# Score masking and its row maxima in one pass per head, and a reordered gating piece, in a two-layer hybrid decoder kernel

## The reference

```python
h = rms_norm(x, norm1)
z = h @ w_in                       # split into za, bq, bk, bv, cq, ck, cv, cg
a_out = causal_spatial_gating(gelu(za), a_ln_g, a_ln_b, a_ws, a_bs)
b_out = dilated_attention(bq, bk, bv)        # 8 heads of 64
c_out = silu(cg) * groupnorm(retention(rotary(cq), rotary(ck), cv))
x = x + concat(a_out, b_out, c_out) @ w_out
x = x + hier_moe(rms_norm(x, norm2), ...)    # 16 experts of 3 x 2 MB, fp32

def causal_spatial_gating(z, ...):           # z = gelu(za)
    u, v = split(z)
    vn = layer_norm(v) * ln_g + ln_b
    s = tril(w_s) @ vn + b_s                 # over 128 tokens, 4 groups
    return u * s
```

## Time and profile before

| | us |
|---|---|
| median of 3 executions | 717.48 |
| lowest, highest | 714.62, 717.77 |
| span of the profiled execution | 714.6 |

### The profile page before, as it was taken

The page is one execution under the profiler, slowest core; times in us unless marked ns, Lnnn a source line. Parts: engine busy times, 40 slices in busy tenths (PEclk is TensorE's granted clock), DMA queues, the critical chain, the costliest instruction groups (busy, mean ns, idle before and its releaser), DMA issues.

```text
span 714.6 us, 9124 instructions
## 1 busy us (share of the span) xinstructions
PE 670.8 (94%) x3452; PEld 384.6 (54%) x3452; DVE 308.9 (43%) x605; ACT 191.9 (27%) x342; POOL 16.3 (2%) x29
## 2 busy tenths in 40 slices
PE   6998999999999999998999989999999999999984
PEld 5877778733543543542388768785353453453431
DVE  3479886711331321321474798865131331231224
ACT  3438434311201201201154445442111111111102
POOL 3000000200000000000020000000000000000000
PEclk9999999999999999999999999999999999999998
DMA  9974039999999999999986330898999999999991
GB/s 334 341 276 168 1 137 389 372 421 404 422 406 394 422 421 421 421 421 421 402 285 223 130 118 30 328 389 338 424 403 423 403 423 415 421 422 419 421 414 63
DMA packets 46026, 240.95 MB, mean 337 GB/s; under 512 B 3457, under 2 KB 3649, under 8 KB 21281
## 3 DMA queue, kind: packets, MB, share of 16 engines
q1 hardware_dynamic: 44800, 238.21, 82.8%
q0 software_dynamic: 1040, 2.04, 1.1%
q10 hardware_dynamic: 144, 0.13, 0.1%
HBM read 239.32 MB, written 1.05 MB: 336 GB/s over the span
## 4 chain that ended last, share of the span: by engine, by line
PE 74%; DMA 10%; DVE 8%; ACT 4%; issue 2%; SPq 1%; DVEq 0%; PEldq 0%; ACTq 0%
PE psum L1059 28%; PE psum L746 14%; PE psum L1091 14%; DMA up_w<-in_w_up 7%; PE psum L1043 4%; DMA down_w<-in_w_in 3%; PE psum L1004 3%; PE psum L766 2%; ACT xT L671 1%; PE psum L973 1%; DVE scores L1200 1%; PE psum L1071 1%; PE psum L914 1%; PE psum L731 1%; DVE scores L1182 1%
## 5 line engine op out<-in xcount | busy, mean ns | idle before, releaser
L746 PE MATMUL psum<-piece_hi,hT_part 128*128 128x512 f32 x416 | 130.2, 394 | 3.4 <-ACT gate_b L611 1.5
L1059 PE MATMUL psum<-up_w,xT 128*64 128x512 f32 x512 | 113.3, 594 | 4.9 <-DMA up_w<-in_w_up 4.9
L1091 PE MATMUL psum<-down_w,scores 128*64 128x512 f32 x512 | 113.5, 595 | 0.6 <-ACT scores L680 0.6
L746 PEld LDWEIGHTS psum<-piece_hi,hT_part 128*128 128x128 f32 x416 | 76.7, 188 | 21.0 <-issue 5.8
L746 PE MATMUL psum<-piece_lo,hT_part 128*128 128x512 f32 x208 | 81.2, 391 | 0.0
L1059 PEld LDWEIGHTS psum<-up_w,xT 128*64 128x64 f32 x512 | 37.7, 137 | 76.7 <-issue 68.2
L1091 PEld LDWEIGHTS psum<-down_w,scores 128*64 128x64 f32 x512 | 36.6, 137 | 64.7 <-issue 63.1
L1495 DVE TENSOR_TENSOR y_lo<-psum,y_hi 128x512 fp32r<-128x512 f32 x32 | 22.1, 691 | 110.9 <-ACT y_hi L687 110.9
L1059 PE MATMUL psum<-gate_a,xT 128*64 128x512 f32 x256 | 56.6, 593 | 1.2 <-DMA gate_a<-in_w_gate 1.2
L1059 PE MATMUL psum<-gate_b,xT 128*64 128x512 f32 x256 | 56.4, 593 | 0.0
L1474 DVE SCALAR_TENSOR_TENSOR work<-work,psum 128x512 f32<-128x512 f32 x16 | 11.0, 687 | 100.8 <-ACT work L678 100.8
(11 more groups left out here) (234 smaller groups left out, 763.2 us busy)
## 6 DMA issues: line engine op xcount, KB each, us to landing
up_w<-in_w_up SPq DMA_DIRECT2D x32, 2048.0 KB, 13.7
down_w<-in_w_down SPq DMA_DIRECT2D x64, 1024.0 KB, 11.7
gate_b<-in_w_gate SPq DMA_DIRECT2D x32, 1024.0 KB, 13.0
gate_a<-in_w_gate SPq DMA_DIRECT2D x32, 1024.0 KB, 15.9
up_w<-in_w_in SPq DMA_DIRECT2D x6, 2048.0 KB, 13.4
down_w<-in_w_in SPq DMA_DIRECT2D x4, 2048.0 KB, 21.3
down_w<-in_w_out SPq DMA_DIRECT2D x4, 2048.0 KB, 7.8
up_w<-in_w_in SPq DMA_DIRECT2D x4, 1024.0 KB, 8.4
```

The lines of the kernel that those rows point to most:

```text
L746: ins = pe.matmul(o, src[a][:, c, t * P:(t + 1) * P], w[b][:, c, :], start=(c == 0 and n == 0), stop=(c == DC - 1 and n == len(parts) - 1))
L1059: ins = pe.matmul(psum[e * SLOTS:(e + 1) * SLOTS, bank, :], xT[:, c, k:k + SLOTS], w[:, e, c, :], start=(c == 0), stop=(c == DC - 1))
L1091: ins = pe.matmul(psum[e * SLOTS:(e + 1) * SLOTS, 2 + n, :], heT[:, c, e * SLOTS:(e + 1) * SLOTS], down_w[:, e, c, n * COLS:(n + 1) * COLS ...
```

## The change

- `mask` and `score_max` become one: for each head and token tile one `tensor_tensor_reduce` that adds a table to the products, multiplies by `q_scale`, writes `scores`, and keeps the minimum of what it wrote. `q_scale` is now negative, so that `scores` hold the negated masked scores and the minimum is the negated maximum. The exponentials take `scale=-1.0`. The table `logq` is `logc` divided by the (positive) scale, made once per layer by two instructions, with `q_inverse` (one small instruction) for it.
- `masked` is signalled by each of the eight instructions instead of once, and the eight exponentials each wait for their own.
- ScalarE takes `exps(0)` ahead of the tanh of the gating piece; `split_hi(CVG)` follows the tanh.
- VectorE takes `norm_probs(0)` right behind `gelu_arg`, ahead of the wait for the tanh; `split_lo(CVG)` goes ahead of the layer norm's statistics; the cosines go ahead of the wait for the spatial product; `split_lo(BV, 0)` goes behind `mask(1)`.
- TensorE does the spatial product in the middle of CVG (in `swap_score`) instead of ahead of it.

```diff
+        q_inverse = sb("q_inverse", [P, T])
+        logq = sgate.rearrange("p t n -> p (t n)")[:, 0:3 * P]
-        scored, masked, exped = signal("scored", 2), signal("masked", 2), signal("exped", 2)
+        scored, masked, exped = signal("scored", 2), signal("masked", 16), signal("exped", 2)
...
-                    act.wait_ge(masked.sem, masked.at(l, k + 1))
                     for j in heads:
-                        act.activation(scores[:, j, 0:P], scores[:, j, 0:P], ACT.Exp, bias=nmax[:, k, j:j + 1],
+                        act.wait_ge(masked.sem, masked.at(l, 8 * k + 2 * j + 1))
+                        act.activation(scores[:, j, 0:P], scores[:, j, 0:P], ACT.Exp, bias=nmax[:, k, j:j + 1], scale=-1.0,
                                        accum_out=denom[:, k, j:j + 1])
+                        act.wait_ge(masked.sem, masked.at(l, 8 * k + 2 * j + 2))
...
+                exps(0)
                 act.wait_ge(gelu_arg.sem, gelu_arg.at(l, 1))
                 act.activation(work1[:], work0[:], ACT.Tanh, ...).then_inc(gelu_tanh.sem, 1)
-                exps(0)
                 split_hi(CVG)
...
-                pe.wait_ge(vn_ready.sem, vn_ready.at(l, 1))
-                for g in range(4):
-                    ins = pe.matmul(psum[:, 7, :]..., wsT[:, g, :], za[...], start=True, stop=True)
-                ins.then_inc(spatial_done.sem, 1)
                 def swap_score():
+                    pe.wait_ge(vn_ready.sem, vn_ready.at(l, 1))
+                    for g in range(4):
+                        ins = pe.matmul(psum[:, 7, :]..., wsT[:, g, :], za[...], start=True, stop=True)
+                    ins.then_inc(spatial_done.sem, 1)
                     pe.wait_ge(proj_copied_a.sem, proj_copied_a.at(l, CQK))
...
-                pe.wait_ge(masked.sem, masked.at(l, 2))
+                pe.wait_ge(masked.sem, masked.at(l, 16))
...
-                    for b in range(2):
-                        link(V.scalar_tensor_tensor(scores[:, 2 * b:2 * b + 2, 0:P], ...))
-                    for b in range(2):
-                        link(V.scalar_tensor_tensor(scores[:, 2 * b:2 * b + 2, P:3 * P], ...))
-                def score_max(k):
-                    link(V.tensor_reduce(nmax[:, k, 0:4], scores[:, :, 0:P], AX.X, ALU.max, negate=True))
-                    V.tensor_reduce(nmax[:, k, 4:8], scores[:, :, P:3 * P], AX.X, ALU.max, negate=True).then_inc(masked.sem, 1)
+                    for j in range(4):
+                        cols = slice((j % 2) * P, (j % 2 + 1) * P)
+                        V.tensor_tensor_reduce(out=scores[:, j, 0:P], in0=psum[:, 6 + j // 2, cols], in1=logq[:, 0:P], scale=q_scale[:, 0:1],
+                                               scalar=-3 * NEG, op0=ALU.add, op1=ALU.min, accum_out=nmax[:, k, j:j + 1]).then_inc(masked.sem, 1)
+                        cols = slice((j % 2) * SEQ, (j % 2 + 1) * SEQ)
+                        V.tensor_tensor_reduce(out=scores[:, j, P:3 * P], in0=psum[:, 4 + j // 2, cols], in1=logq[:, P:3 * P], scale=q_scale[:, 1:2],
+                                               scalar=-3 * NEG, op0=ALU.add, op1=ALU.min, accum_out=nmax[:, k, 4 + j:5 + j]).then_inc(masked.sem, 1)
...
-                V.tensor_scalar(q_scale[:], rstd[:, 0:T], HD ** -0.5, None, ALU.mult).then_inc(rstd_in_ready.sem, 1)
+                V.tensor_scalar(q_scale[:], rstd[:, 0:T], -HD ** -0.5, None, ALU.mult).then_inc(rstd_in_ready.sem, 1)
+                link(V.scalar_tensor_tensor(q_inverse[:], rstd[:, 0:T], HD ** 0.5, meansq[:, 0:T], ALU.mult, ALU.mult))
...
+                V.tensor_scalar(logq[:, 0:P], C("logc")[:, 0:P], q_inverse[:, 0:1], None, ALU.mult)
+                link(V.tensor_scalar(logq[:, P:3 * P], C("logc")[:, P:3 * P], q_inverse[:, 1:2], None, ALU.mult))
                 split_lo(ZA, 0)
...
-                score_max(0)
+                norm_probs(0)
                 dve.wait_ge(gelu_tanh.sem, gelu_tanh.at(l, 1))
                 link(V.scalar_tensor_tensor(zf, work1[:], 1.0, zf, ALU.add, ALU.mult))
+                split_lo(CVG, 0)
+                split_lo(CVG, 1)
...
                 link(inverse_roots(T, link))
-                norm_probs(0)
...
                 ins.then_inc(vn_ready.sem, 1)
-                split_lo(CVG, 0)
-                split_lo(CVG, 1)
+                dve.wait_ge(proj_copied_a.sem, proj_copied_a.at(l, CQK))
+                V.tensor_tensor(rot[:], qkc[:], C("cos")..., ALU.mult).then_inc(cos_done.sem, 1)
                 dve.wait_ge(spatial_done.sem, spatial_done.at(l, 1))
...
-                dve.wait_ge(proj_copied_a.sem, proj_copied_a.at(l, CQK))
-                V.tensor_tensor(rot[:], qkc[:], C("cos")..., ALU.mult).then_inc(cos_done.sem, 1)
-                split_lo(BV, 0)
...
                 mask(1)
-                score_max(1)
+                split_lo(BV, 0)
                 copy_piece(CVG, vgc[:, 1, :], rstd_in[:, 1:2])
```

More of the change, by code:

```diff
@@ L310, in hybrid_trunk @@
         scattered, x_added = signal("scattered", 4), signal("x_added", 4, 3)
-        VSTEPS = 132
+        VSTEPS = 124
         v_step = signal("v_step", VSTEPS)
@@ L560, in exps @@
                 def exps(k, heads=range(4)):
-                    act.wait_ge(masked.sem, masked.at(l, k + 1))
                     for j in heads:
-                        act.activation(scores[:, j, 0:P], scores[:, j, 0:P], ACT.Exp, bias=nmax[:, k, j:j + 1],
+                        act.wait_ge(masked.sem, masked.at(l, 8 * k + 2 * j + 1))
+                        act.activation(scores[:, j, 0:P], scores[:, j, 0:P], ACT.Exp, bias=nmax[:, k, j:j + 1], scale=-1.0,
                                        accum_out=denom[:, k, j:j + 1])
+                        act.wait_ge(masked.sem, masked.at(l, 8 * k + 2 * j + 2))
                         ins = act.activation(scores[:, j, P:3 * P], scores[:, j, P:3 * P], ACT.Exp,
-                                             bias=nmax[:, k, 4 + j:5 + j], accum_out=denom[:, k, 4 + j:5 + j])
+                                             bias=nmax[:, k, 4 + j:5 + j], scale=-1.0, accum_out=denom[:, k, 4 + j:5 + j])
                     if j == 3:
@@ L869, in _ @@
                 turn_tokens(1, PIECE_BANK[CQK])
-                pe.wait_ge(vn_ready.sem, vn_ready.at(l, 1))
-                for g in range(4):
-                    ins = pe.matmul(psum[:, 7, :].rearrange("p (t n) -> p t n", t=T)[:, :, g * HD:(g + 1) * HD], wsT[:, g, :],
-                                    za[:, :, A_W + g * HD:A_W + (g + 1) * HD], start=True, stop=True)
-                ins.then_inc(spatial_done.sem, 1)
-                def swap_score():
+                def swap_score():
+                    pe.wait_ge(vn_ready.sem, vn_ready.at(l, 1))
+                    for g in range(4):
+                        ins = pe.matmul(psum[:, 7, :].rearrange("p (t n) -> p t n", t=T)[:, :, g * HD:(g + 1) * HD], wsT[:, g, :],
+                                        za[:, :, A_W + g * HD:A_W + (g + 1) * HD], start=True, stop=True)
+                    ins.then_inc(spatial_done.sem, 1)
                     pe.wait_ge(proj_copied_a.sem, proj_copied_a.at(l, CQK))
@@ L1292, in _ @@
                 ins.then_inc(vn_ready.sem, 1)
-                split_lo(CVG, 0)
-                split_lo(CVG, 1)
+                dve.wait_ge(proj_copied_a.sem, proj_copied_a.at(l, CQK))
+                V.tensor_tensor(rot[:], qkc[:], C("cos").unsqueeze(1).to_broadcast([P, 4, SEQ]), ALU.mult).then_inc(cos_done.sem, 1)
                 dve.wait_ge(spatial_done.sem, spatial_done.at(l, 1))
@@ L1302, in _ @@
                                        ALU.mult, ALU.mult).then_inc(gated_a.sem, 1)
-                dve.wait_ge(proj_copied_a.sem, proj_copied_a.at(l, CQK))
-                V.tensor_tensor(rot[:], qkc[:], C("cos").unsqueeze(1).to_broadcast([P, 4, SEQ]), ALU.mult).then_inc(cos_done.sem, 1)
-                split_lo(BV, 0)
                 partner = work1.rearrange("p (c t) -> p c t", c=4)
```

7 lines of the change are left out of this document (removed).

## The result

Median of the changed kernel: 709.91 us (708.90 to 711.25, 6 runs), against 717.62 us for the kernel before in the same measurement (714.62 to 719.08, 6 runs, three of them those known ahead of the prediction). The ratio is 0.9895, 95% interval 0.9875 to 0.9915: 7.5 us less. A second measurement on another occasion (e8) gave 0.9901, 0.9881 to 0.9921. The forecast was 5.0 us less, 712.5.

What follows compares the result with a forecast made beforehand. TensorE was taken to bound the mixing half, stalled by VectorE, and the weight stream the expert half. Two layers at 2.5 us gave 5.0 us, from a median of 717.48 to 712.5 us; range 709.2 to 716.3.

Steps and rivals of the forecast that it cites:

- the most that can be won: TensorE's three waits in the mixing stretch, 1.67 + 0.71 + 0.32 = 2.70 us per layer, 5.4 us in all.
- Mask: Fusing mask and maxima on VectorE: four pairs take 3.6 us against 4.5, so 0.9 us less per group.
- p: Time of one pair of fused mask reductions (128 and 256 columns) on VectorE: 0.90 us, ends 0.70 and 1.04.
- First half: From the first mask to score(1): the 1.67 and 0.71 us waits go, and score(1) starts 2.38 us earlier.
- The margin of 0.2 us at score(1): `gated_a` at 71.9 us was to come 0.2 us before TensorE ends its swap at 72.1.
- One for one: What TensorE gains ahead of BV's end moves the whole weight stream and the end equally, in each of two layers.
- Small additions: `q_inverse` and `logq` on VectorE, 0.7 us, fit into a wait for ScalarE; uncovered, up to 0.9 us per layer.
- 1: A new TensorE wait (late `vn_ready` or dearer mask at `retain`) takes part of the gain: 714.5 us; chance 0.22.
- 2: The fused reduction runs at half rate, a pair takes 1.3 us, 0.5 us won per layer: 716.4 us; chance 0.05.
- 3: The gain stays in the mixing half, since the weight stream's end doesn't follow its start: 717.5 us; chance 0.10.
- 4: Each custom VectorE instruction pays a start of its own; at 1.6 us a pair, 721.5 us, slower; chance 0.05.

Runs made afterwards that it cites:

- e8: The changed kernel itself, measured again on another occasion against the kernel before; 0.9901 of the kernel before.
- e4: The changed kernel with four more reductions, each waited for, ahead of each mask (some 2.0 us more VectorE work per mask); 0.9953 of the kernel before.
- e7: The changed kernel with `split_lo(CVG)` put back behind the layer norm; 0.9978 of the kernel before.
- e10: The changed kernel with the cosines back behind `gated_a` and `split_lo(BV, 0)` back ahead of `mask(1)`; 0.9938 of the kernel before.
- e1: The kernel before plus only the fused mask and its table, all other steps in the old order; 0.9961 of the kernel before.
- e3: The changed kernel with the spatial product put back ahead of CVG; 1.0070 of the kernel before.
- e2: The changed kernel with the old mask, its separate maxima and one signal for all eight exponentials; 1.0022 of the kernel before.
- e5: The changed kernel with the first expert's half of `up_w` loaded already after CVG's projection, the second's after BV's; 0.9900 of the kernel before.
- e6: The changed kernel with the first load of `up_w` held until the attention's last product; 0.9922 of the kernel before.
- e9: The changed kernel with ScalarE taking the tanh ahead of the first exponentials again; 1.0020 of the kernel before.

## Why the prediction was right, and where it was off

The direction and the mechanism were right: VectorE's queue held TensorE at the places named, and the change took every one of these waits away. In their place came only one of 0.16 us per layer, too short to be printed. The size was 5.0 us and came out at 7.3 to 7.5, above the 5.4 that the text called the most that can be won. The measured 709.91 us lies in the stated range (709.2 to 716.3) by luck: the low end was the lowest execution before, 714.62, less 5.4, and with the median in its place it would have been 712.1. Point by point:

**Mask.** The term p was 0.90 and measured 0.68, just under the low end of 0.70. The read of the accumulator overlaps with the next reduction, which a single instruction behind which something waits can't show. This moved `decayed` from a forecast 87.6 to 86.05 us, so that TensorE, not VectorE, comes last at `retain`: 2.7 instead of 2.5 us per layer by the forecast's own terms. VectorE is ahead there by 0.2 us only, and e4 shows that it is the next bound.

**First half.** Division done at 56.1 (forecast 57.0), `vn_ready` at 67.3 (68.4), spatial product at 68.8 (69.3), score(1) 2.87 us earlier, of which 0.36 were there at the start of the mask; forecast 2.38. The margin of 0.2 us at score(1) was not there: `gated_a` comes at 70.76 + 0.69 = 71.45 us, the swap's 1.80 us would be over at 71.44, and score(1) starts at 71.60, so that the swap has 1.96 us. It has 1.95 to 1.96 in e4, e7 and e10 too, which have the same order, and 1.81 in e1 and e3, where the spatial product is ahead of CVG. (The forecast took the statistics to start at 57.12; the trace has 57.15, which changes nothing.) The 0.71 us ahead of CVG were rightly given to `split_lo(CVG, 0)`, not to the copy that the row names: e7 has the same wait and names `piece_lo`.

**"The most that can be won".** This is the step that failed: 1.67 + 0.71 + 0.32 = 2.70 us per layer were the idle times of three rows, and 49.65 - 46.02 = 3.63 were won (3.69 in layer 1). Two terms were missing. The rows of the kernel before that show it, next to those of the earlier trace rows, are these of TensorE and ScalarE:

```profile
72.67 1.88 PE L880 MATMUL psum<-gate_b,const 128*128 128x512 f32 x4
74.47 0.49 PE L798 MATMUL psum<-gate_b 64*128 64x128 f32 x4
...
83.19 0.66 PE L836 MATMUL psum<-const,h 128*128 128x128 f32 x4
84.10 0.70 PE L746 MATMUL psum<-piece_hi,hT_part 128*128 128x512 f32 x2 [0.26 <-issue]
```

```profile
83.33 0.67 ACT L551 ACTIVATE vgc<-psum,rstd_in 128x512 f32<-128x512 f32 x1
```

From start to start, layer 0, in us:

| from, to | before | after | won | idle printed before |
|---|---|---|---|---|
| first mask instruction, `turn_probs(0)` | 12.72 | 10.90 | 1.82 | 1.67 |
| `turn_probs(0)`, CVG; with the spatial product | 4.13 | 2.37 + 0.88 | 0.88 | 0.71 |
| first half of CVG | 5.53 | 5.56 | -0.03 | |
| swap, to score(1) | 1.80 | 1.96 | -0.16 | |
| score(1), `turn_mix` | 8.72 | 8.69 | 0.03 | |
| `turn_mix`, BV | 0.91 | 0.41 | 0.50 | 0.26 |
| first half of BV, to `retain` | 6.05 | 5.57 | 0.48 | 0.32 |
| `retain`, first expert load | 9.79 | 9.68 | 0.11 | |
| sum | 49.65 | 46.02 | 3.63 | 2.96 |

- The idle time of a row understates what a stall costs. The rows give a matmul 0.39 us, but in a full row of them one starts every 0.23 us (24 in 5.5 us); idle time is counted from the modelled end, 0.16 us after the next could have started. The four stalls cost 0.15 to 0.24 us more each than is printed, 0.72 in all. In e7 one stall of 1.81 cost 2.05, in e10 one of 1.17 cost 1.27 (47.29 - 46.02).
- There was a fourth stall, 0.26 us ahead of BV, which the waits put down as "issue"; I left it out because it was called so. BV waits for two copies of CVG, ScalarE's and VectorE's. Before the change ScalarE's came last, at 84.00, because it stood behind exponentials that waited for the maxima, and BV began at 84.10. e1, with the fused mask alone, has both copies start at 80.66 and no stall. e2 and e4 have one at the same place (0.64 and 0.73 us), but there VectorE's copy came last (83.52 and 81.99, BV at 83.73 and 82.21), although e2's row names ScalarE's.

Against these 0.26 and 0.72, and 0.11 behind `retain`, stand the 0.16 us lost at score(1).

**What passes to the end.** One for one, as forecast, but not for the reason given. The text said that the stream of weights sets the expert stage and that its start moves it. e5 and e6 speak against this: an earlier start brings nothing, and 6.0 us of delay in each layer cost 1.5 in both together. The gain passes, as I read it, because TensorE is the main bound there too, and all loads behind its events move with it; that is argued from e5, e6 and the busy times, and no run shows it by itself. Over the runs the stretch and the time agree within some 1.6 us (e1 -3.3 and -2.8, e2 +2.0 and +1.6, e3 +3.9 and +5.0, e4 -2.6 and -3.4, e7 -3.2 and -1.6, e9 +0.7 and +1.4, e10 -4.8 and -4.4, each against before).

**Small additions.** `logq` took 0.6 us in layer 1 and left 0.76 of the 1.15 us of waiting: covered, as forecast. No time for a table change appears between exponentials and tanh.

**Rivals.** 1: a new wait did come, `gated_a` ahead of score(1), but of 0.16 us; the margins were as thin as stated, or thinner (e4, e10). 2: the reduction runs at about 1.1 ns a column (0.41 less 0.27 over 128 columns), not at half rate. 3: fell as a rival, the gain reached the end, although its doubt about the stream's start was justified. 4: no start cost.

What stays open: what the signal for each head and the shorter mask are worth apart; the 95% intervals leave the split between 7.1 and 7.5 undecided, and why e7's executions scatter over 8 us isn't explained. e7's profile is of one of its quicker executions (713.39 against a median of 715.78), which is most of why stretch and time differ there.

## What to carry to other kernels

Where one engine's queue feeds several waits of the bounding engine, price the edits together: here the cheap mask alone gave 2.8 us, the order alone lost 1.6, both gave 7.5, and undoing a step or two of the order cost between 2.7 and 12.5. Bound a gain by the start-to-start distances of the bounding engine's instructions, not by the sum of the idle times printed, and follow up each short stall that the profile calls "issue" to what it ended on: all that the instruction waits for, and which of it came last. A DMA share of 1.0 alone doesn't make the stream the bound; delay it and see.

## What the runs showed of the hardware that I had not expected

- A reduction with an accumulator read, followed by another that doesn't wait for it, steps at 0.27 us for 128 columns and 0.41 for 256; the read (0.08 us) overlaps. Waited for, 0.40 and 0.52.
- TensorE standing still for 3.92 us was followed by some 3 us at the lower clock (0.50), which made a stall of 3.9 us cost 5.5. Stalls of 0.97 and 2.00 us 8 us apart were followed by it in one layer and not in the other (e9). The stalls of the kernel before in this stretch, up to 1.69 us, were followed by none, nor was e7's of 1.81.
- The weight stream ran at a DMA share of 1.01 both at 414 and at 421 GB/s.
